# Second layer's q and k of fourteen heads as block pairs by seven products, kept in DRAM until the heads

## The reference

```python
def _fox_mixer(xn, w_in, b_f, q_norm, k_norm, w_out):
    proj = xn @ w_in
    q, k, v, f_pre, z = jnp.split(proj, [...], axis=-1)
    q = _rmsnorm(heads(q), q_norm); k = _rmsnorm(heads(k), k_norm); v = heads(v)
    c = jnp.cumsum(log_sigmoid(f_pre + b_f))
    s = q k^T * 128**-0.5 + (c_q - c_k), masked to kpos <= qpos
    o = softmax(s) v
    y = o * silu(z)
    return y @ w_out
```

## Time and profile before

| | us |
|---|---|
| median of 3 runs | 2919.91 (2917.34 to 2921.38) |
| the profiled execution, its own time | 2919.34 |
| its span | 2917.4 |
| PE busy | 2833.5 (97% of the span) |
| PE weight loads busy (beside PE) | 2694.1 (92%) |
| DVE busy | 1903.2 (65%) |
| ACT busy | 1225.3 (42%) |
| POOL busy | 225.5 (8%) |

### The profile page before, as it was taken

How to read it: one execution, slowest core, us unless ns; L and a number is a source line. 1 busy time by engine, 2 the same in 40 slices (tenths; PEclk the granted TensorE clock), 3 DMA queues, 4 the chain that set the end, 5 groups by cost and what they waited for, 6 DMA issues and landing times. The chain is left out here.

```text
span 2917.4 us, 52635 instructions
## 1 busy us (share of the span) xinstructions
PE 2833.5 (97%) x20861; PEld 2694.1 (92%) x20861; DVE 1903.2 (65%) x2587; ACT 1225.3 (42%) x1599; POOL 225.5 (8%) x319
## 2 busy tenths in 40 slices
PE   6999999999999999999999999999999999999997
PEld 6899999999999999999999999898898998998786
DVE  7999999996564666656678889454554544544532
ACT  5444444445553433434343444433433434334322
POOL 0000000000001211122200000000000000000121
PEclk9999999999999999999999999999999999999998
DMA  4344444446564444444535545222222222222322
GB/s 172 131 146 144 149 140 147 139 158 241 214 225 156 158 167 159 139 156 155 170 124 183 179 145 188 101 83 87 76 94 76 76 94 76 77 92 76 132 86 86
DMA packets 87289, 393.51 MB, mean 135 GB/s; under 512 B 10880, under 2 KB 12032, under 8 KB 63008
## 3 DMA queue, kind: packets, MB, share of 16 engines
q1 hardware_dynamic: 60288, 277.98, 27.2%
q0 software_dynamic: 26704, 114.17, 11.7%
q10 hardware_dynamic: 208, 0.14, 0.0%
HBM read 326.35 MB, written 65.90 MB: 134 GB/s over the span
## 5 line engine op out<-in xcount | busy, mean ns | idle before, releaser
L2284 PE MATMUL mm<-xl,w_hi 128*128 128x264 f32 (+1 forms) x1824 | 502.6, 334 | 2.9 <-DVE w_lo L1377 1.7
L2284 PE MATMUL mm<-xh,w_hi 128*128 128x264 f32 (+1 forms) x1824 | 497.6, 331 | 4.7 <-DVE xl L1389 3.7
L2284 PE MATMUL mm<-xh,w_lo 128*128 128x264 f32 (+1 forms) x1628 | 466.0, 332 | 0.0
L1377 DVE TENSOR_TENSOR w_lo<-w_raw,w_hi 128x2048 fp32r<-128x2048 f32 x133 | 304.5, 2290 | 86.2 <-ACT w_hi L803 86.2
L2333 PE MATMUL mm<-xq,w_hi 128*128 128x264 f32 x2112 | 345.7, 285 | 0.0
L2284 PEld LDWEIGHTS mm<-xh,w_hi 128*128 128x128 f32 x1824 | 304.6, 188 | 40.3 <-DVE xl L1389 3.5
L2284 PEld LDWEIGHTS mm<-xl,w_hi 128*128 128x128 f32 x1824 | 302.7, 188 | 34.1 <-issue 3.2
L803 ACT ACTIVATE w_hi<-w_raw 128x2048 fp32r<-128x2048 f32 x133 | 253.7, 1907 | 127.9 <-PE mm L2284 117.9
L2284 PEld LDWEIGHTS mm<-xh,w_lo 128*128 128x128 f32 x1628 | 276.2, 189 | 30.3
L2333 PEld LDWEIGHTS mm<-xq,w_hi 128*128 128x128 f32 x2112 | 293.5, 189 | 0.5
L2384 PE MATMUL mm<-s,w_hi 128*128 128x264 f32 x1344 | 246.5, 284 | 5.0 <-DVE w_lo L1409 5.0
(11 more groups left out here) (411 smaller groups left out, 6097.1 us busy)
## 6 DMA issues: line engine op xcount, KB each, us to landing
w_raw<-in_weights_dram SPq DMA_DIRECT2D x132, 1024.0 KB, 4.8
w_raw<-in_slots_dram SPq DMA_DIRECT2D x184, 512.0 KB, 3.7
xm_scratch<-pad POOLq DMA_DIRECT2D x32, 264.0 KB, 3.1
xc_whole<-xc_scratch SPq DMA_DIRECT2D x8, 1056.0 KB, 6.8
xm_whole<-xm_scratch SPq DMA_DIRECT2D x8, 1056.0 KB, 5.0
qk_scratch<-qkv POOLq DMA_DIRECT2D x8, 1056.0 KB, 11.7
qk_whole<-qk_scratch POOLq DMA_DIRECT2D x8, 1056.0 KB, 5.2
xc_load<-xc_scratch POOLq DMA_DIRECT2D x32, 264.0 KB, 3.7
```

The source lines that it names most:

```text
L1377: dve.tensor_tensor(w_lo[par_][:, :], w_raw[par_][:, :], w_hi[par_][:, :].bitcast(F32), ALU.subtract).then_inc(w_lo_ready, 1)
L2284: i = pe.matmul(ps[:, at:at + n], w, v[:, t0:t0 + n], start=first and k == 0, stop=last and k == 2)
```

## The change

Heads 0 and 1 keep their q and k as plain blocks, but now ahead of the head loop: k0, q1 and k1 follow `two_blocks`. The q and k blocks of each of the other 14 heads become one pair of seven products. The products need x in quarters and four new sums of quarters: POOL reads the stored sum h back into quarters (`load_quarters`), ACT multiplies by the layer's norm weights (`gained`) and rounds the sums (`high_sums`), DVE forms them (`sums_h`) and their low parts (`lows_h1`, `lows_h2`). The unsummed operands are the tiles of x that lie there already (`h_operand`). DVE makes the weight sums and joins the products as in the other pairs. POOL stores each pair's q and k (and the plain ones) to DRAM. They are stored without RT. SP loads half blocks, four for a pair.

`head_b1` then has two blocks, v and z. POOL reads a head's q and k back in one transfer of 128 rows of 1040 floats (`load_qk4`), issued after the low parts of the previous head's k and q (`hat_lo`), and DVE multiplies them by RT in place, at the start of its iteration. On PE the v and z blocks are cut into pieces, with scores, transposes and the sums of squares between them; the sums come after 10 of z's 16 tiles, and DVE and ACT normalize and split k and q before they touch z and v. After the loop comes `round_w` and `low_w` of the second output block.

Beside this, PE gets small matmuls of 128 columns whose results nobody reads (`keep_running`): 3 at each of four waits and 8 at each of four places before the first opening step, and 10 before the first opening step of pass f = 1.

```diff
-    B1_PER = 4
     B1_0 = Z_LAST + CT
-    B2_0 = B1_0 + 1 + BH * B1_PER
+    PLAIN = 2
+    VZ_0 = B1_0 + 1 + 2 * PLAIN
+    B2_0 = VZ_0 + 2 * BH
     BLOCKS = B2_0 + KT
+    QK_PAIRS = BH - PLAIN
...
+    def qk_prod(n, i):
+        return out_step(2, 0) + PRODUCTS * n + i
+
+    def qk_pair(n):
+        return out_pair(2, n)
+
+    def qk_ring(g):
+        return at_ring(g + 2)
...
+                j, t0 = (k if i == 0 else HK + k), (HT if i == 6 else 0)
+                return at_tile(HIGH_AT[j])[:, t0:t0 + HT], at_tile(LOW_AT[j])[:, t0:t0 + HT]
+            return tuple(s[:, k, :] for s in OPERANDS[i])
+
+        XT = [t.rearrange("p (q n) -> p q n", n=HT) for t in (sq_two[:, :], rb_first[:, :])]
...
+            for n in range(QK_PAIRS):
+                for j, free in ((0, 1), (1, 4), (3, 5), (2, 6)):
+                    if n == 0:
+                        sp.wait_ge(w_lo_ready, VZ_0 if j < 2 else VZ_0 - 1)
+                    else:
+                        sp.wait_ge(slot_lo, qk_prod(n - 1, free) + 1)
+                    load_slot(SLOTS_OUT + 2 * OUT_SLOTS + 4 * n + j, j)
...
+            def load_quarters(k0, k1):
+
+                for half in range(2):
+                    for t in range(2):
+                        src = h_d.rearrange("p (j t n) -> p j t n", t=2, n=HT)[:, half * HK + k0:half * HK + k1, t, :]
+                        pool.dma_start(x0[:, 2 * half + t, k0:k1, :], src).then_inc(x21_loaded, 16)
...
+            for i in range(2):
+                pool.wait_ge(rb_stored[i], 16 * HK)
+            load_quarters(HK // 2, HK)
...
+            for n in range(QK_PAIRS):
+                for done in (c11_ready, c22_ready, c12_ready, c21_ready):
+                    pool.wait_ge(done, qk_pair(n) + 1)
+                pool.dma_start(qk4_d[PLAIN + n], QK_OUT[n % 2][:, :]).then_inc(qk_stored4(n)[0], 16)
+
+            def load_qk4(h):
+                pool.dma_start(QKR[:, :], qk4_d[ds(h, 1), :, META:2 * T].rearrange("a p n -> (a p) n")).then_inc(qk_loaded, 16)
...
+            load_qk4(0)
+            for n in (QK_PAIRS - 2, QK_PAIRS - 1):
+                pool.wait_ge(*qk_stored4(n))
             pool.dma_start(negc_b[:, :], negc_d[0:1, :].broadcast_to([P, T])).then_inc(negc_loaded, 16)
             with pool.Fori(1, BH) as h:
+                pool.wait_ge(hat_lo, h * 2)
+                load_qk4(h)
                 pool.wait_ge(sadd, h * NT)
                 pool.dma_start(negc_b[:, :], negc_d[ds(h, 1), :].broadcast_to([P, T])).then_inc(negc_loaded, 16)
 
...
+                for half in range(2):
+                    j = half * HK + k
+                    act.activation(XT[k % 2][:, 2 * half:2 * half + 2, :], x0[:, 2 * half:2 * half + 2, k, :], ACT.Copy,
+                                   scale=par[:, C_BN + j:C_BN + j + 1]).then_inc(xt_ready, 1)
...
+            def high_sums(k):
+                act.wait_ge(s_ready, 12 * HK + 4 * k + 4)
+                for a in range(2):
+                    act.activation(SQ[:, 2 * a:2 * a + 2, k, :], SR[:, 2 - 2 * a:4 - 2 * a, k, :], ACT.Copy).then_inc(x_hi, 1)
...
+            gained(0)
+            gained(1)
             act.wait_ge(sumsq_done, 2)
             inv_sqrt(halves(ax[0]), RT[:, :], 1.0 / D, rtmp[:, :], AH + 2, two, ln_ready, rstd_ready)
...
+                dve.tensor_tensor(r1, a21, a22, ALU.subtract).then_inc(s_ready, 1)
+                dve.tensor_tensor(r3, a11, a21, ALU.subtract).then_inc(s_ready, 1)
...
+                if k == 1:
+                    low_w(B1_0 + 3, 1)
+                lows_h1(k)
+                if k + 3 < HK:
+                    sums_h(k + 3)
+                if k == 5:
+                    low_w(B1_0 + 4, 0)
...
+                dve.wait_ge(qk_loaded, h * 16 + 16 * (AH + 1))
+                dve.tensor_tensor(QR, QR, RT[:, META:T], ALU.mult).then_inc(qkv4_ev, 1)
+                dve.tensor_tensor(KR, KR, RT[:, :], ALU.mult).then_inc(qkv4_ev, 1)
                 if attend:
                     for i in range(3):
                         softmax_in(p_, i)
-                low_w(b + 2, q0 % 2)
+                low_w(b + 1, 1)
                 if attend:
...
+            spare = ax[1][:, 0:P]
+            pe.wait_ge(ones_ready, 1)
+            for k in range(4, HK):
+                pe.wait_ge(sq0_ready, k)
+                keep_running(spare, 3)
             pe.wait_ge(sum0_ready, HK)
             full_sum(ax[0], rtmp, HT).then_inc(sumsq_done, 1)
+            keep_running(spare, 8)
+            for ready, value in ((ln_ready, 1), (rstd0_ready, 2), (xt_ready, 2)):
+                pe.wait_ge(ready, value)
+                keep_running(spare, 8)
             for k in range(HK):
...
+                elif f:
+                    keep_running(ax[1][:, BANK:BANK + P], 10)
...
+            pe.wait_ge(f_row, 1)
+            blockmm(B1_0 + 2, 0, mm[1])
+            pe.wait_ge(ev_first, 4 + 1)
+            blockmm(B1_0 + 3, 1, mm[0], REAL)
+            pe.wait_ge(ev_first, 4 + 2)
...
+                for i in range(PRODUCTS):
+                    if n == 0 and i in (1, 2, 4, 5):
+                        pe.wait_ge(s_lo, 5 + 2 * (HK + 2) + HK + {1: 0, 2: 0, 4: 1, 5: 2}[i])
...
+                    for k in range(HK):
+                        at = slice(cols.start + k * P, cols.start + (k + 1) * P)
+                        high, low = h_operand(i, k)
+                        for a, (wt, x) in enumerate(((w_hi, high), (w_hi, low), (w_lo, high))):
+                            j = pe.matmul(BANKS[i], wt[w][:, at], x, start=k == 0 and a == 0,
+                                          stop=k == HK - 1 and a == 2)
+                    j.then_inc(prod_done, 1)
...
-            def head_b1(h, proj, attend, p_, first=False):
-                b = h * B1_PER + (B1_0 + 1)
-                q0 = B1_0 + 1
-                if proj and not first:
+            def head_b1(h, attend, p_):
+                b = h * 2 + VZ_0
+                if attend:
                     pe.wait_ge(ln4_ready, h * 2 - 1)
-                    blockmm(b, q0 % 2, mm[0], REAL)
+                blockmm(b, 0, mm[0], ALL, None, range(0, 5))
                 if attend:
                     pe.wait_ge(hat_lo, p_ * 2 + 2)
                     pe.wait_ge(v4_lo, p_ * 2 + 2)
                     pe.wait_ge(ln4_ready, p_ * 2 + 2)
                     for i in range(3):
                         scores(p_, i)
-                if proj:
-                    if first:
-                        pe.wait_ge(f_row, 1)
-                    else:
-                        pe.wait_ge(gate4_ready, h)
-                    blockmm(b + 1, (q0 + 1) % 2, mm[1])
+                blockmm(b, 0, mm[0], ALL, None, range(5, 12))
                 if attend:
                     pe.wait_ge(sadd, p_ * NT + 2)
                     scores(p_, 3)
+                blockmm(b, 0, mm[0], ALL, None, range(12, KT))
+                if attend:
+                    pe.wait_ge(sadd, p_ * NT + 3)
                     transpose_p(p_, 0)
-                if proj:
-                    pe.wait_ge(sq4_ready, h * 2 + 1)
-                    blockmm(b + 2, q0 % 2, mm[0])
+                    transpose_p(p_, 1)
+                    pe.wait_ge(qkv4_ev, h * 4)
+                blockmm(b + 1, 1, mm[1], REAL, None, range(0, 4))
                 if attend:
+                    pe.wait_ge(pt_lo, p_ * (NT + 1) + 1)
+                    transpose_p(p_, 2)
                     pe.wait_ge(sadd, p_ * NT + 4)
-                    transpose_p(p_, 1)
-                    pe.wait_ge(pt_lo, p_ * (NT + 1) + 1)
-                    for n in range(2, NT + 1):
-                        transpose_p(p_, n)
-                if proj:
-                    pe.wait_ge(sq4_ready, h * 2 + 2)
-                    blockmm(b + 3, (q0 + 1) % 2, mm[1], REAL)
-
-                    pe.wait_ge(qkv4_ev, h * 4 + 3)
-                    full_sum(mm[0], sq[1], HT).then_inc(sum4_done, 1)
-                    if attend:
-                        pe.wait_ge(pt_lo, p_ * (NT + 1) + (NT + 1))
-                    for a in range(NT):
-                        m = pe.matmul(ax[0][:, a:a + 1], sq[0][:, a * P:(a + 1) * P], ones[:, 0:1], start=True, stop=True)
-                    m.then_inc(sum4_done, 1)
+                    transpose_p(p_, 3)
+                blockmm(b + 1, 1, mm[1], REAL, None, range(4, 8))
+                if attend:
+                    transpose_p(p_, 4)
+                blockmm(b + 1, 1, mm[1], REAL, None, range(8, 10))
+                pe.wait_ge(sq4_ready, h * 2 + 2)
+                pe.wait_ge(qkv4_ev, h * 4 + 3)
+                full_sum(mm[0], sq[1], HT).then_inc(sum4_done, 1)
+                if attend:
+                    pe.wait_ge(pt_lo, p_ * (NT + 1) + 4)
+                for a in range(NT):
+                    m = pe.matmul(ax[0][:, a:a + 1], sq[0][:, a * P:(a + 1) * P], ones[:, 0:1], start=True, stop=True)
+                m.then_inc(sum4_done, 1)
+                blockmm(b + 1, 1, mm[1], REAL, None, range(10, KT))
                 if attend:
```

(18 more changed lines are left out.)

371 lines of the change are left out of this document (289 added, 82 removed).

## The result

| kernel | median us | lowest to highest | runs |
|---|---|---|---|
| before | 2919.52 | 2917.34 to 2921.38 | 4 |
| changed | 2875.97 | 2875.54 to 2880.53 | 4 |

The ratio is 0.9857 with a 95% interval of 0.9845 to 0.9870: 43.6 us less by the medians. The forecast, 37.5 less, was set against the profiled execution of the kernel before (2919.34); the changed kernel's took 2876.11 us, 43.2 less. Its span is 2874.6.

A forecast was written before the change was run, and what follows sets the result against it. PE, busy 97% of the span, was taken as the bound. The terms summed to -37.5 us against the profiled 2919.34, giving 2881.8, say 2882 us, with a range of 2875 to 2899.

The forecast's parts named there:

- The pairs: q and k of 14 heads: 22.83 us each give way to a pair of 20.30, -35.4 us in all.
- The turn of a head: Head loop: an iteration loses q and k, 54.07 to 31.24 us, with PE still setting it.
- The softmax chain: Head loop: DVE's softmax and PE's transposes both reach 16.8 us after v's start, even, loss 0.
- The ring of the reload: Head loop: q's low part, load, RT multiply, softmax, transposes to sums take 30.0 us, 1.2 below 31.24.
- A: Head loop: softmax or a slower reload sets the head, 6 to 20 us more, about 2895; chance 0.21.
- B: Head loop: reload as slow as a large POOL load; each microsecond above 5.5 costs 15, up to 2973; chance 0.05.
- The way in: Before the first pair: PE idles 1.4 us ahead of q1 and 1.6 ahead of k1, +2.6 us.
- Head 0 and the tail: Head 0's wait -1.3, head 1's late q +1.6, behind the loop -2.1, up to 2 more if the clock stays up.
- The start: Before k of head 0: -2.9 us (-2.0 - 1.4 + 0.5), of it -2.0 from small matmuls at the first steps.
- Pass f = 1: Its first opening step: ten small matmuls shorten the gap to about 2.5 us and hold the clock, -1.4 us.
- The loads of quarters: POOL's queue at 1816: four loads (2.1 MB) crowd the last load of h, +0.5 us.
- Rival C: First steps and pass f = 1: clock not held, +3.4 us, 2885; chance counted within the forecast's 0.62.

The follow-up runs named there:

- e1_before_split: Kernel before, with only the last group of attention transposes (4 of 14) issued after z's first four row tiles: 2911.43 us, ratio 0.9975.
- e10_lump: Changed kernel with the last group of transposes moved four row tiles of z earlier, making one lump of 11: 2877.52 us, ratio 0.9867 to the kernel before.
- e7_reload_late: Changed kernel with three unused GpSimd additions per head turn ahead of issuing the q and k reload: 2907.66 us, ratio 0.9956 to the kernel before.
- e3_z_early: Changed kernel with the third and fourth transpose groups two row tiles of z earlier on PE: 2893.52 us, ratio 0.9912 to the kernel before.
- e2_no_dummies: Changed kernel without any `keep_running` matmuls, the waits kept: 2873.81 us, ratio 0.9849 to the kernel before.
- e11_again: The changed kernel itself, unedited, measured once more on another chip: 2878.39 us, ratio 0.9870 to the kernel before.
- e9_all: Changed kernel with DVE's new order before the pairs and clock-holding matmuls at 942, 1479, the head loop's end and 2670 us: 2869.79 us, ratio 0.9832 to before.
- e6_tail: Changed kernel with twice 20 clock-holding matmuls at the head loop's end, before the last scores and the projection's first block: 2876.44 us, ratio 0.9850 to before.
- e5_keep_gates: Changed kernel with 16 clock-holding matmuls at layer 1's first scores (placed behind the wait) and 16 before the output projection's second step: 2878.94 us, ratio 0.9861 to before.
- e8_no_reload: Changed kernel without the q and k load in the head loop, heads 1 to 15 reusing the buffer: 2877.11 us, ratio 0.9854 to the kernel before.

## Why the prediction was right where it was, and where not

- **The pairs.** Right: 20.36 for 20.30, and DVE has 16.02 of it where the forecast came to about 15. 14 x 0.06 is 0.8 us of gain less. By the formula of the Trainium skill ("TensorE: Matmul & The Clock Gate", Back-to-back issue gap), which that section gives for an isolated matmul, a pair is estimated at 18.9; the trace has 121 ns a matmul again and not 112.5, so the rows were the better price.
- **The turn of a head.** The step that failed is "an iteration loses q and k: 54.07 - 22.83 = 31.24". The attention remainder of 8.37 was carried over as if it were all PE work, but 0.42 of it was a wait inside the lump of transposes, which the change divides (e1_before_split, e10_lump). A turn is 0.45 less than forecast; this term is 6.75 us for 15 turns, more than the whole miss of 5.7. It stood in the trace: 13 transposes in 1.8 us, where 1.42 is what they take without a wait.
- **The chains.** The softmax chain, "even" in the forecast, had 0.57 us of room. The ring of the reload had 1.2 by the forecast and 0.7 by e7_reload_late. The ring less its load was sized 5.0 + 1.4 + 12.8 + 6.5 = 25.7; e7_reload_late has 32.61 - 7.1 = 25.5 (7.1 is from the end of q_low to the start of q). The load landed after 3.8 us where 4.3 was taken. Rivals A and B did not occur. A lay 0.6 us away: e3_z_early makes the softmax chain the bound and comes out at 2893.5, where A had "about 2895". B's slope, one microsecond a turn for each beyond the room, is what e7_reload_late shows (1.82 for 2.53).
- **The way in.** +1.6 for +2.6. The two idle times were named with their cause and place. The first is 1.16 for 1.4; of the second only 0.32 was there for 1.6, because DVE had the low part of k1 at 1868.4 and not at 1870.1.
- **Head 0 and the tail.** Right in kind: -1.1 for -1.3, +1.1 for +1.6, and -2.8 for -2.1 behind the loop. PE idles 2.21 and 2.16 us there, for the "about 2.3" forecast, and the clock did not stay up (granted 0.66 over 2655 to 2665), so the "up to 2 more" is not in it.
- **The start.** Here the forecast failed: by the start of k of head 0 there is -0.3 for -2.9. "The first steps run at 122 ns" is wrong: 18 or so of them still ran at the low clock, and the lead was 1.2 us and not 2.0. Nothing of it arrived. The fall at 942 took more than all of it (0.83 granted in the window row above), and the late store at 1479 took 1.3 more, so the last pair ahead of pass f = 1 ended 1.3 us later than before. The forecast had neither of the two.
- **Pass f = 1.** There PE waits for a load of y in both kernels. Chain of waits, before and changed:

```profile
1634.54 8.71 DMA x_f<-y_scratch
```
```profile
1635.86 6.95 DMA x_f<-y_scratch
```

It was issued 1.3 us later and took 1.8 less, so the first step starts at 1645.61 for 1646.04. The loss was hidden by that, and not by the wait: the load is issued behind PE's own work, and in e2_no_dummies and e11_again, where it took 7.0 and 7.2, it was issued at 1633.84 and 1637.91 and the first step started at 1643.67 and 1647.87. Why it takes 6.6 to 8.9 us from profile to profile is not shown. The first step then ran at the full clock, as forecast (third window row; the pass's first pair is 1.8 us ahead of before, a step of 1.3 for 1.4). That the ten matmuls did this is not shown: in e2_no_dummies, without them, PE idles 1.43 us there, and its first twelve matmuls run at the full clock too (1.68 us, where the kernel before took 2.98).
- **The loads of quarters.** Between the pairs of pass f = 1 and k of head 0, two idle times of PE ahead of weight blocks are 0.74 and 1.57 us, for 0.85 and 0.39 before, which took 1.1 back. ACT waits 2.88 us there for a load of h, where it waited 1.52. In e11_again the two idle times are 0.48 and 0.49. So the crowd of quarter loads, if it is the cause, costs from nothing to 1.1, where 0.5 was taken.
- **The rivals at the small matmuls.** Rival C ("the small matmuls change nothing") fits what e2_no_dummies shows for the whole run. At the start they did give a lead, 1.2 us, which was lost again behind it.

The forecast missed by two opposite errors: a gain of 6.8 in the turns that it did not see, and 2.6 of gain ahead of the heads that did not come. That the sum lands within 6 us owes something to luck. The median, 2875.97, lies below the forecast's own bracket (2877 to 2887), in the case "better than 2877" with its chance of 0.04. One of that case's two reasons, a smoother way in, gave 1.0 us; the other, the tail's clock, did not come, and the main reason, the turn, was not named. e11_again, 2878.39, lies within the bracket.

## What to carry to other kernels

Before a remainder is carried over, take it apart into instructions times their price: what is left over is a wait, and a new order may remove it. A group that needs another engine's answer to the group just ahead of it should stand some work away from it. Matmuls that only hold the clock brought something here only in e9_all, where nearly every idle time of about 2 us was filled, ahead of its wait. Judge them by the whole run, since they move everything behind them, the fetches of instructions too.

## What the hardware showed that was not expected

- At one idle time of 2.2 to 2.3 us the clock fell in six profiles and not in seven. It fell in all five in which it had first risen by 32.7 us, 900 us earlier, and in one of the eight in which it rose later. A fall to 1.2 GHz took 1.5 to 1.9 us. With several such places this may be most of why runs of one kernel lie 4 to 7 us apart; e9_all, with most of these places filled, has 3.
- One idle time of 1.44 us had a fall behind it (e9_all at 1645) and one of 1.43 at the same place had none (e2_no_dummies), while 2.60 us behind the head loop had none in the kernel before and in the changed one, but one in e6_tail.
- In e5_keep_gates PE ran its 16 matmuls without a gap behind 2.24 us of idle time, and the low clock still lasted longer than in the changed kernel (granted 0.50 over 945 to 950, for 0.76), in the stretch whose matmuls have 16 output rows.
- With 44 short matmuls more at the start of PE's program a fetch of 16 KB of instructions came at 1475 us and not at 1482, beside a store of 264 KB, which landed after 3.6 us for 2.3. In the changed kernel's two profiles it landed after 3.6 and 4.6.
- An added load of 520 KB in each turn cost PE nothing: without it the turn stays at 30.79 us (e8_no_reload).
